# Interleaving a projection with its convolution, moving the last right sides and the decays of a recurrence

## The reference, cut to what matters

```python
x = first_block(x, ...)                       # ends with rmsnorm(x, norm_final)
p_ctx = _modulate(ctx, sh1c, sc1c) @ w_in     # 256 context tokens
p_lat = _modulate(x, sh1, sc1) @ w_in         # 512 latent tokens
# the first CONV_CH = 2560 columns: a 3-tap convolution along the context, a 3x3 one on the grid of 8 x 64 latent tokens
mq, mk, rr, rk, rv, mv, mo, gates, lw_f, lw_b, la, lg = jnp.split(u, SPLIT_POINTS, axis=-1)
out_m = _mlstm_group(...)    # chunkwise recurrence with input and forget gates, both directions
out_r = _rwkv7_group(...)    # per step: state = state*w - removed*(kh*a) + v*k ; y = state @ r, both directions
x = _layernorm(ALPHA * x + g1 * (concat(out_m, out_r)[latent] @ w_out), ln1_g, ln1_b)
ffn = _hier_moe(...)         # 32 experts, 2 of one group of 8 per token
```

## Time and profile before

| | us |
|---|---|
| median of 3 runs (lowest, highest) | 3076.74 (3072.43, 3082.67) |
| the profiled execution's own time | 3069.58 |
| its span in the trace | 3067.8 |
| mean granted clock of TensorE over the span | 0.969 |
| busy: TensorE, VectorE, ScalarE, GpSimd | 2844.1, 1843.4, 1268.2, 779.9 |

### The profile page before, as it was taken

One profiled execution on the slowest core, in us unless ns is written; L12 is line 12 of the kernel. 1 busy time (PEld: TensorE's weight loads), 2 busy tenths in 40 slices (PEclk: granted clock), 3 DMA queues, 4 the chain that ended last, 5 costly groups with the idle time before them and its releaser, 6 DMA issues. The chain is left out here.

```text
span 3067.8 us, 54455 instructions
## 1 busy us (share of the span) xinstructions
PE 2844.1 (93%) x22521; PEld 2299.8 (75%) x22521; DVE 1843.4 (60%) x2599; ACT 1268.2 (41%) x1624; POOL 779.9 (25%) x411
## 2 busy tenths in 40 slices
PE   9889999999999999999979899868998699999994
PEld 7467888789777777888858687567885478888883
DVE  3766553110344445555156966775754789999997
ACT  3544332132233334322244321423332267777775
POOL 2013444443322213444410000000000124444431
PEclk9999999999999999999999899889999799999997
DMA  4633522232211112222222110141003389999997
GB/s 170 236 136 111 97 99 97 96 136 84 81 70 68 58 56 96 97 96 96 96 83 110 55 36 12 65 175 45 31 18 122 131 309 361 373 372 372 365 369 271
DMA packets 83394, 440.91 MB, mean 144 GB/s; under 512 B 19712, under 2 KB 22784, under 8 KB 34816
## 3 DMA queue, kind: packets, MB, share of 16 engines
q1 hardware_dynamic: 73920, 429.63, 38.6%
q0 software_dynamic: 9280, 8.43, 0.8%
HBM read 423.30 MB, written 37.77 MB: 150 GB/s over the span
## 5 line engine op out<-in xcount | busy, mean ns | idle before, releaser
L85 POOL TENSOR_TENSOR ring_lo<-ring,unit_hi 128x2048 fp32r<-128x2048 f32 x110 | 507.3, 4612 | 1044.1 <-ACT unit_hi L74 1044.1
L146 PE MATMUL wide<-h_hi,unit_hi 128*128 128x512 f32 x1296 | 515.7, 398 | 13.2 <-DVE h_lo L566 5.0
L148 PE MATMUL wide<-h_hi,ring_lo 128*128 128x512 f32 x1296 | 507.1, 391 | 0.0
L147 PE MATMUL wide<-h_lo,unit_hi 128*128 128x512 f32 x1296 | 506.3, 391 | 0.0
L3343 DVE TENSOR_TENSOR ex_w_lo<-ring,ex_w_hi 128x2048 fp32r<-128x2048 f32 x194 | 442.3, 2288 | 41.3 <-ACT ex_w_hi L3338 40.0
L3338 ACT CAST ex_w_hi<-ring 128x2048 fp32r<-128x2048 f32 x194 | 369.4, 1907 | 113.9 <-DMA ring<-in_weights 103.6
L74 ACT CAST unit_hi<-ring 128x2048 fp32r<-128x2048 f32 x114 | 217.7, 1909 | 387.6 <-PE wide L148 382.4
L146 PEld LDWEIGHTS wide<-h_hi,unit_hi 128*128 128x128 f32 x1296 | 244.6, 189 | 73.8 <-issue 15.2
L148 PEld LDWEIGHTS wide<-h_hi,ring_lo 128*128 128x128 f32 x1296 | 244.3, 188 | 52.3
L147 PEld LDWEIGHTS wide<-h_lo,unit_hi 128*128 128x128 f32 x1296 | 244.8, 189 | 49.1 <-issue 0.2
L391 DVE TENSOR_TENSOR ffn_hidden_lo<-ffn_whole,ffn_hidden_hi 128x512 f32 (+1 forms) x44 | 201.3, 4576 | 51.0 <-ACT ffn_hidden_hi L366 51.0
(11 more groups left out here) (560 smaller groups left out, 5587.1 us busy)
## 6 DMA issues: line engine op xcount, KB each, us to landing
ring<-in_weights SPq DMA_DIRECT2D x356, 1024.0 KB
rw_F<-factors SPq DMA_DIRECT2D x9, 1024.0 KB, 5.7
factors<-rp_out SPq DMA_DIRECT2D x4, 1280.0 KB, 5.3
factors<-rp_out SPq DMA_DIRECT2D x4, 1024.0 KB, 5.0
ex_both<-pair_rows_out SPq DMA_DIRECT2D x4, 1024.0 KB, 7.9
x<-in_x SPq DMA_DIRECT2D x8, 256.0 KB, 6.1
x_kept<-x SPq DMA_DIRECT2D x1, 2048.0 KB, 12.4
x<-x_kept SPq DMA_DIRECT2D x1, 2048.0 KB
```

The source lines that it names most:

```text
L85: pool.tensor_tensor(self.lo[n % RING][:, :], self.ring[n % RING][:, :], self.hi[n % 2][:, :].bitcast(F32), ALU.subtract).then_inc(self.lo ...
L146: pe.matmul(dst, a[0], b[0], start=start, stop=False)
L147: pe.matmul(dst, a[0], b[1], start=False, stop=False)
L148: return pe.matmul(dst, a[1], b[0], start=False, stop=stop)
```

## The change

In the entry, TensorE transposes the power of x (four small transposes), so that its inverse root is a value for each partition: `c.x_cols`, four columns, times ALPHA. The routing stage uses these columns as the scale of its ScalarE copy, and x itself gets only the norm's gain, now by eight ScalarE activations after item 1 is copied. GpSimd clears the grids. The low part of unit 0 is written ahead of the variance, the root of the variance is taken before that of the power.

In the projection the items come in another order, `PROJECTED`, and the weights are packed on the host in that order:

```diff
-    items = [("mixed", 0), ("lw", 0), ("lg", 0)] + [("mo", m) for m in range(MC)] + [("conv", m) for m in range(CONV_CHUNKS)]
+PROJECTED = [("mixed", 0), ("lw", 0), ("conv", 0), ("conv", 1)]
+for m, kind in enumerate(("mo", "mo", "mo", "mo", "lg")):
+    PROJECTED += [(kind, m % MC), ("conv", m + 2)]
+PROJECTED += [("conv", m) for m in range(7, CONV_CHUNKS)]
-GATES_AT = 1
+GATES_AT = 6
```

Items 0 and 1 are computed together: first both context parts, then both latent parts chunk by chunk. ScalarE writes the high part of unit u + 2 as soon as unit u is used. The values rotate through the banks in another order, 6, 7, 0, 1, 2, 3, so that they wait for 26 copies and not 27:

```diff
+            unit = w.parts(pe, 0, 0)
+            pe.wait_ge(entry.loaded, 16 * len(entry.loads))
+            for n in range(2):
+                for k in range(DC):
+                    block(n, unit, k, con(n), context)
+            for k in range(DC):
+                pe.wait_ge(entry.h_lo_ready, k + 1)
+                for n in range(2):
+                    mm = block(n, unit, k, lat(n), latent)
...
-            pe.wait_ge(copied, len(items))
+            pe.wait_ge(copied, len(items) - 1)
...
-                if n >= 2 and n % 2 == 0:
-                    w.write_hi(act, 0, n // 2 + 1)
+                if n % 2 == 1:
+                    w.write_hi(act, 0, n // 2 + 2)
...
-                if m == 0:
-                    w.write_lo(dve, 0, 4)
-                elif m == CONV_CHUNKS - 2:
-                    w.write_lo(dve, 0, U_IN_COLUMNS)
-                elif m % 2 == 1 and m < CONV_CHUNKS - 1:
-                    w.write_lo(dve, 0, (m + 9) // 2)
+                while following <= min((n + 1) // 2 + 1, U_IN_COLUMNS):
+                    w.write_lo(dve, 0, following)
+                    following += 1
```

In the factors' stage the decays move from VectorE to GpSimd, where they stand ahead of the three copies:

```diff
+                step = chain_of(pool, gain_step)
+                for d in range(2):
+                    pool.wait_ge(edges_ready, N - 1 + d)
+                    step(pool.tensor_tensor(f.gain[:, d, :, :], edges[:, d, 1, :, :], edges[:, d, 0, :, :], ALU.subtract))
...
-                    if i == N - 1:
-                        dve.wait_ge(edges_ready, N - 1)
-                        gain(0)
...
-                dve.wait_ge(edges_ready, N)
-                gain(1)
```

In the recurrence, for the last tile, `turn_hidden` moves from slot 14 to 11 and `mix_hidden` from 16, 17 to 12, 13; `chain` parts 0 and 1 with their copies move into slots 14 to 17. The outputs are begun in the banks of the inverse (`LAST_Y`), which are free by then. VectorE makes the copies of direction 1, ScalarE those of direction 0:

```diff
-                pe.wait_ge(mixed_ready, MC)
-                for part in range(2):
-                    for d in both:
-                        chain(TAT - 1, d, part)
                 first_outputs(TAT - 1)
+                last_output_begun(0)
                 rest_of_base(TAT - 1)
+                last_output_begun(1)
                 rest_of_outputs(TAT - 1)
                 for d in both:
-                    chain(TAT - 1, d, 2)
+                    last_output_ended(d)
...
-                for part in range(6):
-                    for d in both:
-                        carry(TAT - 1, d, part)
+                for part in range(2, 6):
+                    carry(TAT - 1, 0, part)
```

More of the change, by code:

```diff
@@ L1261, in tensor @@
             pe.matmul(self.c.bank[4], self.c.ones[:, :], self.sq[:, k % 2, :], start=(k == 0), stop=(k == DC - 1)).then_inc(self.square_summed, 1)
+        pe.wait_ge(self.power_ready, 1)
+        for t in range(TT):
+            mm = pe.transpose(self.c.bank[7][:, t * P:(t + 1) * P], self.x_scale[:, t * P:(t + 1) * P], self.c.ident[:, :])
+        mm.then_inc(self.power_turned, 1)
     def scalar(self, act, between):
@@ L1499, in _, with block @@
             entry.tensor(pe)
+            def block(n, unit, k, dst, toks):
+                b = (n % 2 * DC + k) * P
+                return product(pe, dst, [part[:, b:b + P] for part in unit], [part[k][:, toks] for part in h], k == 0, k == DC - 1)
+            latent, context = slice(CTX, TA), slice(0, CTX)
+            unit = w.parts(pe, 0, 0)
[3 more added lines that the diff above has]
+                    block(n, unit, k, con(n), context)
+            for k in range(DC):
+                pe.wait_ge(entry.h_lo_ready, k + 1)
+                for n in range(2):
+                    mm = block(n, unit, k, lat(n), latent)
+                    if k == DC - 1:
+                        mm.then_inc(w.used if ends[n] else chunk_done, 1)
             for n, (kind, m) in enumerate(items):
+                if n < 2:
+                    continue
                 if n % 2 == 0:
                     unit = w.parts(pe, 0, n // 2)
+                if n == 3:
+                    pe.wait_ge(entry.power_root_ready, 1)
                 if n >= 4:
                     pe.wait_ge(copied, n - 3)
-                parts = [(lat(n), slice(CTX, TA))]
-                if kind in ("mixed", "lw") or kind == "conv" and not latent_only(m):
-                    parts.append((con(n), slice(0, CTX)))
+                parts = [(lat(n), latent)] + ([(con(n), context)] if kind == "conv" and not latent_only(m) else [])
                 for dst, toks in parts:
-                    if n == 0 and toks.start == 0:
-                        pe.wait_ge(entry.loaded, 16 * len(entry.loads))
                     for k in range(DC):
-                        if n == 0 and toks.start == CTX:
-                            pe.wait_ge(entry.h_lo_ready, k + 1)
-                        b = (n % 2 * DC + k) * P
-                        mm = product(pe, dst, [part[:, b:b + P] for part in unit], [part[k][:, toks] for part in h], k == 0, k == DC - 1)
+                        mm = block(n, unit, k, dst, toks)
                 mm.then_inc(w.used if ends[n] else chunk_done, 1)
-            pe.wait_ge(copied, len(items))
+            pe.wait_ge(copied, len(items) - 1)
             for k in range(DC):
@@ L1527, in _ @@
                     mm.then_inc(w.used, 1)
+            pe.wait_ge(copied, len(items))
             gates.tensor(pe, c)
@@ L2492, in rest_of_outputs, with last_output_begun, last_output_ended @@
                                 mm.then_inc(u_done[d], 1)
+                def last_output_begun(d):
+                    p, t = TAT - 1, tile(TAT - 1, d)
+                    for m in range(MC):
+                        for a in both:
+                            pe.matmul(LAST_Y[d][half[a], m * P:(m + 1) * P], S[d][half[a], m, :], F(p, d)[half[a], m, 1, :], start=m == 0, stop=False)
+                    for m in range(MC):
+                        for a in both:
+                            pe.matmul(LAST_Y[d][half[a], m * P:(m + 1) * P], r.vtm[:, t, head(d, 2 * m + a)], G[1 - p % 2][:, d, 2 * m + a, 3 * P:4 * P],
+                                      start=False, stop=False)
+                def last_output_ended(d):
+                    p = TAT - 1
+                    pe.wait_ge(u_ready[d], 2 * p + 2)
+                    for m in range(MC):
+                        for a in both:
+                            mm = pe.matmul(LAST_Y[d][half[a], m * P:(m + 1) * P], U[d][:, 2 * m + a, :], G[1 - p % 2][:, d, 2 * m + a, P:2 * P],
+                                           start=False, stop=m == MC - 1)
+                    mm.then_inc(y_done[d], 1)
                 def turn_hidden():
@@ L2678, in _ @@
                                 scale_hidden(p - 2)
-                            if p == TAT - 1 and at in (16, 17):
-                                for m in range(2 * (at - 16), 2 * (at - 16) + 2):
+                            if p == TAT - 1 and at in (12, 13):
+                                for m in range(2 * (at - 12), 2 * (at - 12) + 2):
                                     mix_hidden(m)
```

135 lines of the change are left out of this document (79 added, 56 removed).

## The result

| | before | after |
|---|---|---|
| median of the runs, us | 3075.24 (6 runs, 3070.72 to 3082.67) | 3053.72 (6 runs, 3043.54 to 3059.53) |
| ratio to before | | 0.9924, 95% interval 0.9911 to 0.9938 |
| profiled execution: time, span, mean granted clock | 3069.58, 3067.8, 0.969 | 3054.79, 3053.0, 0.969 |

The changed kernel is faster by 0.76%, 21.5 us by the medians. The forecast was 3047 with a range of 3034 to 3060: the sign and the range hold, and the gain is 6 us smaller than the 27.9 of the sum.

The account below looks back on a forecast made before the run. TensorE bounds the projection at first, VectorE its later stretch. Projection 20.6, decays 1.3 and tail 6.0 sum to 27.9 us off 3069.6, 3041.7, or 3048.8 from the median; forecast 3047 (70%), range 3034 to 3060.

Parts of the forecast that it names:

- The shared stretch: Projection after item 13: VectorE sets the pace, 106.5 us before the values start at 1789.8; gain 20.6 us.
- items 0 and 1: Projection's start: each input chunk feeds both items, which end at about 1602, where item 0 ended before.
- Rival (a): TensorE's clock stays at 1.2 GHz through the projection's VectorE-paced stretch; kernel slower, about 3132; 3%.
- Rival (b): Waits in the projection's VectorE-paced stretch come in bad places; projection gives only 10 us, 3059; 14%.
- rival (d): VectorE is ahead, its waits already counted in the 152.9 us; TensorE sets the projection's pace: 34 + 7 us, 3035; 9%.
- Decays on GpSimd: Factors' stage before the recurrence: decays leave VectorE, whose last item then waits for stores; gain 1.3 us, bounds -1.5 and +2.
- my sign of being wrong: A stage after GpSimd's decays that begins later against its predecessor than before.
- the low value: GpSimd's twelve small decay steps cost 3 us, not the 14 if each waits out a VectorE operation.
- Tail: Recurrence's end: right sides move into the last two levels, outputs begun in gaps; gain 6.0 us, bounds 2 and 8.
- levels: Last tile's right sides move into the recurrence's last two levels: gain 1.3 us (0 to 2).
- rival (e): Right sides only lengthen the recurrence's last levels, the tail gives 1 us: 3052; no chance given.
- rival (c): The gain is given back later, in the experts' stream; time stays within 9 us of 3077; 4%.

Follow-up runs that it names:

- the execution with the clock up: Changed kernel with ScalarE's eight gains after convolution 0's copies and unit 4's load ahead of the store of x: ratio 0.9928 to before.
- The experiments: Changed kernel with low parts 14 and 15 one convolution earlier (ratio 0.9877 to before), or the last two gate steps behind the last low part (0.9899).
- first pair of profiles: Kernel before and changed kernel, profiled once each: 3069.58 and 3054.79 us; projection, factors and recurrence give 25.4 us.
- the second: Both kernels unchanged, run and profiled again: times 3076.97 before and 3054.85 changed; projection, factors and recurrence give 20.4 us.
- all fourteen profiles: Six profiles with the old projection and eight with the new, from both kernels, their repeats and the experiments' kernels.
- divided copies: Kernel before with the last tile's right sides in the last two levels and the second direction's copies on VectorE: ratio 0.9986, recurrence 316.7 us.
- the two series of the changed kernel: The changed kernel's first runs and its unchanged repeat: ratios to before 0.9924 and 0.9929.
- the decays alone: Kernel before with only the decays moved to GpSimd: 3075.87 us, ratio 1.0004.
- the right sides alone: Kernel before with only the last tile's right sides and their ScalarE copies in the last two levels: ratio 0.9996, recurrence 320.8 us.
- the projection alone: Kernel before with only the interleaved projection, the entry and the scaling by columns: 3058.41 us, ratio 0.9941.
- second profile of before: Kernel before, unchanged, run and profiled again: 3076.97 us, ratio 0.9999; recurrence 318.3 us.

## Why the prediction was right, and where it was off

**The shared stretch.** Forecast: 106.5 us from the first convolution behind item 13 to the low part of unit 14, VectorE-bound. Measured: from 1689.68 to 1795.7, 106.0. The values were forecast 205.0 us behind the reciprocal (1789.8 less 1584.83) and came after 205.8. The projection gave 19.4 us by its own marks, 20.6 forecast. What was off is one assumption: items 0 and 1 were to end 17.2 us behind the reciprocal, and took 18.7 where the clock was down at the entry (17.2 in the execution with the clock up). Rival (a), half the clock, fell: it was 0.96 in the stretch. Rival (b) fell, since the projection gave 19.4 us (18.0 like for like) and not 10, and rival (d) fell, since VectorE was busy 108.2 of 115.9 us and its order set the start of the values.

**What the sum could not see** is that the 106.5 us were a bound only as long as the order in VectorE's queue was kept. I counted all convolutions ahead of low part 14 as work that the values wait for, and noted the idle time of TensorE, but not VectorE's own 20 us of idle time behind it. The experiments moved 8.8 and 5.6 us into it.

**Decays on GpSimd.** Forecast 1.3; 1.0 alone, 0.7 in the first pair of profiles, and 1.8 us lost in the second. Over all fourteen profiles the stage is 173.3 to 174.2 us without and 172.3 to 175.3 with them, with means of 173.9 and 173.7. So no gain is shown, in the stage or in the times (1.0004), and my sign of being wrong, a stage that begins later against its predecessor than before, came in the second profile. Where I took the low value, some 3 us for twelve steps, they took 5.7. In the changed kernel, first GpSimd, then VectorE:

```profile
1988.83 1.05 POOL L2006 TENSOR_TENSOR state_gain<-rp_edges 128x24 f32<-128x24 f32 x1 [22.98 <-ACT rp_edges L2141]
1989.96 2.53 POOL L2009 TENSOR_TENSOR state_gain<-state_gain,rp_edges 128x4 f32<-128x4 f32 x5
```

```profile
1998.19 1.03 DVE L2236 TENSOR_TENSOR rp_out<-conv,rp_down 128x512 f32<-128x512 f32 x1
```

The last item follows its predecessor at once; I had it wait some 0.2 us for a store. (By the sum's own row, 2007.64 and 5.0, that store lands at 2012.6 and not at 2012.3, so the gain should have read 0.95.) But its first operation takes 1.03 us beside GpSimd's copies instead of 0.69, and from its start to the recurrence it is 6.8 us instead of 6.3: 6.7 to 6.9 in the eight profiles with the decays on GpSimd, 6.3 in the six without. So some 0.5 of the 1.5 us taken off VectorE come back, which the sum left out. What made the second profile 1.8 us longer lies ahead of the last item. The steps themselves ended 3.4 us ahead of VectorE's last item and not behind it, so their slowness did not hold it. The Trainium skill's rule (SBUF — State Buffer, "Who interferes with whom") agrees with the slow steps; the 3 us that the sum would have lost by it did not come.

**Tail.** Forecast 6.0 (levels 1.3, the rest 4.7); measured 5.3 in the first pair and 4.1 in the second: levels nothing, the rest 5.4 and 4.5 (15.8 and 15.0 to 10.5, with 11.1 forecast). The mechanism of rival (e) was right for the levels. That the total came near is partly luck: the levels gave none of their 1.3, and the divided copies, to which the sum gave neither cost nor gain, were the largest step, 2.5 us or more. How much the rest gains depends on the clock that the kernel before has in the execution compared.

**The sum.** Forecast 27.9. The medians gave 21.5, and the ratios of the two series of the changed kernel 23.4 and 21.8 (each 4 us to either side). The touched stages gave 25.4 in the first pair of profiles and 20.4 in the second, 22.9 in the mean, which agrees with the times. So the times need no large loss behind the touched stages; what is smaller than forecast is their own gain, mainly the projection's (18.0 to 19.4 for 20.6), the levels' (nothing for 1.3) and the decays' (not shown, for 1.3). The experts' stage was longer by 5.6 and 5.2 us in these profiles, and the way to it and through the entry not the same twice: this part of rival (c), a gain given back later, is not settled. I had also kept for the changed kernel the 7 us by which the profiled execution of before lay below the median. That offset was of this one execution, whose entry and experts' stage were both at the short end; the changed kernel's first profile lies 1.1 us above its median. This is part of why the two spans differ by only 14.8 us.

**What was to show it.** The first convolution came at 1623.8 and not 1618, but with an entry 5.3 us late: 33.7 us behind the reciprocal, 33.2 forecast. TensorE's waits between 1595 and 1680 were 2.9 us for the input's low part and 0.8 for ring_lo, a little over the 3 us; the values came at 1795.9 instead of 1790, for the same late entry; the last addition ended 20.1 us earlier, and not 28, of which those 5.3 us are the largest part.

## What to carry to other kernels

When an engine's sum sets a start, ask which of its work must stand ahead of that start: idle time of the same engine right behind it suggests that the order is the bound, and not the sum. It is a sign to test by moving work behind the start, as here. A one-line rule of when the last weight parts are written was worth 8.8 us of the stage, nearly half of the whole interleaving. And compare kernels stage by stage between marks that both have, in more than one profile of each: one pair of spans differed by 14.8 us where the touched stages gave 25.4, a second by 19.3 where they gave 20.4.

## What the runs showed of the hardware that I had not expected

- **The entry's clock** differs between executions of the same kernel: 16 products at 7.70 us with a granted clock of 1.00, or 10.47 with 0.76.
- **Gaps between small products.** Over 7 us in the last stretch, gaps of 0.88 us went with a clock of 1.00 in the one profile that has them, and gaps of 1.33 us in the same chain with 0.52 to 1.00 (0.52 with the decays alone, 0.56 with the right sides alone, 0.74 in the first profile of before, 0.76 with the projection alone, 1.00 in the second profile of before).
- **A small GpSimd operation beside VectorE.** The first decay step, 24 columns, took 1.05 us in the changed kernel's first profile and 2.72 in its second, while VectorE ran two-input operations of 768 columns back to back; the same step a little later, with VectorE waiting, 0.23. The 2.72 us reach to the end of the third of these operations, at 1992.8. GpSimd and VectorE in order of time, second profile:

```profile
1990.18 2.72 POOL L2006 TENSOR_TENSOR state_gain<-rp_edges 128x24 f32<-128x24 f32 x1 [23.51 <-ACT rp_edges L2141]
...
1994.28 0.23 POOL L2006 TENSOR_TENSOR state_gain<-rp_edges 128x24 f32<-128x24 f32 x1
```

```profile
1990.12 0.95 DVE L2237 TENSOR_TENSOR rp_out<-conv,rp_down 128x768 f32<-128x768 f32 x1
1990.99 0.95 DVE L2238 TENSOR_TENSOR rp_out<-conv,rp_up 128x768 f32<-128x768 f32 x1
1991.86 0.95 DVE L2239 TENSOR_TENSOR rp_out<-conv,rp_up 128x768 f32<-128x768 f32 x1
```
